# A hybrid pooling / RWKV-7 / mixture-of-experts layer on one Trainium2 core: transposes moved to VectorE in the recurrence, expert weights loaded in two halves, gathers and scatters that skip empty rows, and the first two blocks joined

## The reference, cut to what matters

```python
h = modulate(rmsnorm(x, g0), shift, scale)          # shift, scale: silu(c) @ ada_w + ada_b
p = h @ w_in                                        # pool | r, k, v, low-rank w, a, g | two gate logits
# RWKV-7 time mixing, 16 heads of 64, two directions, 256 context + 512 latent tokens:
def step(s, inp):                                   # scanned over the tokens
    sa = einsum('bhvk,bhk->bhv', s, -kk_t)
    s  = s * w_t + sa * b_t + v_t * k_t
    return s, einsum('bhvk,bhk->bhv', s, r_t)
m = (sigmoid(gp) * (pool_y @ pool_proj) + sigmoid(gr) * (rwkv_y @ rwkv_proj)) @ w_out
h = x + gate1 * rmsnorm(m, g1)
# 32 experts in 4 groups: top-1 group, top-2 experts of its 8
y = sum(gates[:, e] * ((silu(u @ w_gate[e]) * (u @ w_up[e])) @ w_down[e]) for e in range(32))
out = h + gate2 * rmsnorm(y, g3)
```

## Time and profile before

| | us |
|---|---|
| three runs | 1523.47, 1524.66, 1525.41 |
| median | 1524.66 |
| the profiled execution | 1523.53 |
| its span (first to last instruction) | 1521.0 |

### The profile page before, as it was taken

How to read it: one execution, slowest core, us unless ns; L and a number is a source line. 1 busy time by engine, 2 the same in 40 slices (tenths; PEclk the granted TensorE clock), 3 DMA queues, 4 the chain that set the end, 5 groups by cost and what they waited for, 6 DMA issues and landing times. The chain is left out here.

```text
span 1521.0 us, 37771 instructions
## 1 busy us (share of the span) xinstructions
PE 1328.0 (87%) x16500; PEld 797.3 (52%) x16500; DVE 620.2 (41%) x974; ACT 578.9 (38%) x964; POOL 235.3 (15%) x191
## 2 busy tenths in 40 slices
PE   5889999999999999999998788999999468788780
PEld 3445555554888888888887233444445323222220
DVE  1247777674555445454444451523321510000014
ACT  4235445542665656556654530000003223322233
POOL 0011111220322333333330000000000011100002
PEclk9999999999999999999999899999999679989895
DMA  9204565645222222112200529453454659999984
GB/s 379 90 1 139 159 174 177 185 123 177 106 86 73 100 67 84 67 71 83 80 29 23 229 99 387 161 202 112 152 219 186 275 214 422 426 424 425 426 341 186
DMA packets 104697, 279.87 MB, mean 184 GB/s; under 512 B 20691, under 2 KB 69971, under 8 KB 90595
## 3 DMA queue, kind: packets, MB, share of 16 engines
q1 hardware_dynamic: 98596, 248.24, 44.0%
q0 software_dynamic: 5952, 29.36, 4.9%
HBM read 232.48 MB, written 53.49 MB: 188 GB/s over the span
## 5 line engine op out<-in xcount | busy, mean ns | idle before, releaser
L391 PE MATMUL pr_ps<-hT,pr_w 128*128 128x512 f32 x384 | 172.2, 602 | 4.0 <-DVEq L99 4.0
L972 DVE COPY_PREDICATED rc_T<-masks_sb,rc_ps 128x512 f32<-128x512 uint32 x96 | 65.2, 728 | 151.2 <-PE rc_ps L761 151.1
L391 PEld LDWEIGHTS pr_ps<-hT,pr_w 128*128 128x128 f32 x384 | 72.1, 191 | 94.9 <-issue 90.1
L1250 PE MATMUL mg_ps<-hT,mg_w 128*128 128x512 f32 x256 | 112.9, 600 | 2.7 <-PEq L1029 2.7
L1737 DVE TENSOR_TENSOR mg_w<-mg_w,ex_pgu 128x256 f32<-128x256 f32 x16 | 6.7, 421 | 194.5 <-ACT mg_w L1731 194.5
L1250 PEld LDWEIGHTS mg_ps<-hT,mg_w 128*128 128x128 f32 x256 | 49.1, 192 | 65.4 <-issue 65.4
L1269 ACT ACTIVATE mg_sig<-mg_ps 128x512 f32<-128x512 f32 x16 | 9.6, 597 | 188.1 <-PE mg_ps L1250 188.1
L761 PE MATMUL rc_ps<-rc_T,rc_Z 64*64 64x64 f32 x3840 | 73.4, 221 | 6.6 <-issue 5.3
L912 ACT ACTIVATE rc_G<-rc_ps 128x512 f32<-128x512 f32 x120 | 66.1, 599 | 23.5 <-PE rc_ps L761 23.0
L501 POOL TENSOR_TENSOR pr_kd<-pr_rate,pool_space 128x768 f32<-128x768 f32 x16 | 29.0, 1814 | 280.9 <-DVE pr_kraw L543 280.9
L734 PE MATMUL rc_ps<-masks_sb,rc_T 128*128 128x128 f32 x480 | 67.6, 281 | 4.8 <-DVE rc_Tf L970 4.8
(11 more groups left out here) (358 smaller groups left out, 2596.7 us busy)
## 6 DMA issues: line engine op xcount, KB each, us to landing
bonus_sb<-in_ada_w SPq DMA_DIRECT2D x16, 1024.0 KB, 7.0
mg_w<-in_w_merge SPq DMA_DIRECT2D x8, 1792.0 KB, 7.5
pr_w<-in_w_prep SPq DMA_DIRECT2D x8, 1664.0 KB, 9.8
kr_chunks<-pr_KR SPq DMA_DIRECT2D x16, 768.0 KB, 4.2
bk_chunks<-pr_BK SPq DMA_DIRECT2D x16, 768.0 KB, 6.5
rc_BK<-bk_chunks SPq DMA_DIRECT2D x24, 512.0 KB, 4.2
rc_KR<-kr_chunks SPq DMA_DIRECT2D x24, 512.0 KB, 4.2
rwkv_y<-in_w_experts SPq DMA_DIRECT2D x5, 2048.0 KB, 17.8
```

What stands on the lines that cost most here:

```text
L391: last = pe.matmul(lat_bank[:, :], wv[:, j * KT + kt, :], hT[:, kt, lat], start=(kt == 0), stop=(kt == KT - 1))
L972: dve.copy_predicated(T[u][:, d, :, :, :].rearrange("p q b t -> p b q t"), level(int(s[1:]), d), by_side).then_inc(dve_s, 1)
L1250: last = pe.matmul(ps[u][j][:, :], w[:, u, w0 + k, :], rhs, start=(k == 0), stop=(k == n - 1))
```

## The change

Three places are changed.

1. `begin` and `low_rank_inputs` become one block. Only the identity is loaded ahead of `ada_w`; the other masks come last. `ada_w` comes in four pieces by rows of the sum (each with all 2,048 columns), so each piece feeds 8 products into four groups of 32 PSUM partitions. One transpose round and one copy bring the columns; the low-rank products start as soon as the first part of `hT` is modulated; and `prepare`'s first loads are issued right behind.
2. In the recurrence T is turned by DVE (`Tt`, one transpose of 128 partitions for d = 0, two of 64 partitions that also swap the halves for d = 1), at every level. The Tr units are gone from PE and ACT. G and X (up to b = 16) and U are made for both directions interleaved. ACT copies both halves of U (DVE copied one before). The turn of V moves behind U.
3. The experts' gate/up and down weights have semaphores of their own and are loaded separately; indirect DMAs carry a bound, and empty rows have an index beyond it; results are scaled by their gate in ACT's copy and scattered to one of two rows per token, so that the end reads them with 8 plain DMAs from SP. The spill loop is entered only if there is a spilled tile. The 8 MB fill is gone.

```diff
@@ begin @@
+                sp.dma_start(g["masks"][:, 0:1, :], I["masks"][:, 0:1, :]).then_inc(ident_loaded, 16)
+                for i in range(PIECES):
+                    sp.dma_start(w[:, i, :, :, :].rearrange("p n k c -> p n (k c)"),
+                                 I["ada_w"][0:NF, :, i * KP:(i + 1) * KP, :].rearrange("n p k c -> p n (k c)")).then_inc(w_loaded[i], 16)
...
+                first_loads(sp)
+                sp.dma_start(g["masks"][:, 1:, :], I["masks"][:, 1:, :]).then_inc(masks_loaded, 16)
...
+                for i in range(PIECES):
+                    pe.wait_ge(w_loaded[i], 16)
+                    for k in range(KP):
+                        for n in range(NF):
+                            pe.matmul(ps[2 * H * n:2 * H * n + 2 * H, :], lhs[:, i * KP + k, :], w[:, i, n, k, :], start=(i + k == 0), stop=False)
@@ recurrence_units @@
-        out += front("G2") + front("Tr1") + front("Vt") + back("P")[0:1] + front("X2") + back("P")[1:2]
-        out += front("G4") + front("Tr2") + back("XTr") + front("X4") + back("U")
-        out += front("G8") + front("Tr4") + back("Y") + front("X8") + back("S") + rows_of(0, 1)
-        out += front("G16") + front("Tr8") + rows_of(2) + front("X16") + rows_of(3)
-        out += front("G32") + front("Tr16") + ahead("BKt") + front("X32")
+        out += front("G2") + back("P")[0:1] + front("X2") + back("P")[1:2]
+        out += front("G4") + back("XTr") + front("X4") + back("U") + front("Vt")
+        out += front("G8") + back("Y") + front("X8") + back("S") + rows_of(0, 1)
+        out += front("G16") + rows_of(2) + front("X16") + rows_of(3)
+        out += front("G32") + ahead("BKt") + front("X32")
@@ recurrence @@
+            by_dve += [("T1", i, d // 2), ("Tt2", i, d // 2)]
+        if s in ("X2", "X4", "X8", "X16") and d == 1:
+            by_dve += [(f"Tt{2 * int(s[1:])}", i, 0), (f"Tt{2 * int(s[1:])}", i, 1)]
...
+                        act.activation(UV[u][0:HD, d, 1::2, :, :], turned[0:HD], ACT.Copy)
+                        act.activation(UV[u][HD:P, d, 0::2, :, :], turned[HD:P], ACT.Copy).then_inc(act_s, 1)
...
+                        for half, to in ((slice(0, P), slice(0, P)),) if d == 0 else zip(OWN, OWN[::-1]):
+                            last = dve.transpose(Tt[u][to, d, :, :, :].rearrange("p q b t -> p (q b t)"), T[u][half, d, :, :, :].rearrange("p q b t -> p (q b t)"))
@@ experts @@
+                for p in range(PAIRS - 2):
+                    sp.wait_ge(s["gu"], p + 1)
+                    for n in (2 * p + WSLOTS, 2 * p + WSLOTS + 1):
+                        if n < NE:
+                            gate_up_of(n)
+                    if p:
+                        sp.wait_ge(s["down"], p)
+                        for n in (2 * p + WSLOTS - 2, 2 * p + WSLOTS - 1):
+                            if n < NE:
+                                down_of(n)
...
+                for t in range(NT):
+                    for j in range(2):
+                        sp.dma_start(got[t][j], g["y_dram"][j * SEQ + t * P:j * SEQ + t * P + P, :]).then_inc(gath[t], 16)
```

486 lines of the change are left out of this document (238 added, 248 removed).

## The result

| | before | after |
|---|---|---|
| median of four runs, us | 1524.07 | 1557.34 (1549.71 to 1572.26) |
| ratio, with its 95% interval | | 1.0234 (1.0156 to 1.0312) |
| the profiled execution | 1523.53 | 1556.44 |
| its span | 1521.0 | 1554.6 |
| mean granted clock of PE | 0.944 | 0.917 |

The account below looks back on a forecast made before the run. Bounds: a start waiting for data, a PE-bound recurrence, a DMA-bound expert stream with a serial end. Terms -11.6 + 30 + 0.9 - 5.6 - 15.5 - 11.6 = -13.4 gave 1511 us; forecast's range 1495 to 1527, wider range 1482 to 1537.

Parts of the forecast that it names:

- The recurrence: Recurrence: DVE and ACT queues replace PE as bound; chunks of 40.5 us latent, 37.3 context; +30 us.
- The layout: Recurrence: step-by-step schedule of one latent chunk over PE, ACT and DVE, 39.2 us without interruptions; 36.0 for context.
- upper bound of +44: Recurrence: the loss if none of the 2 us of interruptions within units hides behind PE's waits.
- Rival 4: Recurrence: DVE and POOL block each other, T1's copies waiting beside POOL's masking; 30 us more, 1541; chance 0.16.
- Rival 1: Recurrence: PE stays the bound, so 60 us go where 30 were added; 1421; chance 0.08.
- rival 2: Recurrence comes out even: new waits swallow all interruptions, hops are shorter; 30 us less, 1481; chance 0.12.
- The start: Start: last `ada_w` piece at 32.3, low-rank products from 39.3 instead of 50.94; gain 11.6 us.
- The merge: Merge: the 8 MB fill vanishes from a PE-bound stage; nothing, or 1 us at most.
- Routing: Routing: two more DVE operations on the way to the first gather; +0.9 us.
- Experts, the stream: Expert stream: earlier reload gains 5.6, empty rows moving nothing 15.5; -28.5 with the end's part before the last pair.
- Rival 3: Experts: empty rows cost as much as full ones, so 15.5 us stay; 1527; chance 0.14.
- The end: Experts' end: later down halves, plain final reads, fewer sums; gain 11.6 in all, -4.2 after the last pair's gate/up begins.

Follow-up runs that it names:

- short waits: Parts 1 and 3 with the old recurrence, PE also waiting after X4, X8, X16 and each G of levels 2 to 32 for their copies: 1549.17 us, 1.0141.
- the version with idle products in the first chunk: Changed kernel with later POOL masks and V's turn back in level 2, plus throwaway identity products in PE's first-chunk waits: 1520.79 us, 0.9936.
- the mended new recurrence: Changed kernel with later POOL masks, V's turn back in level 2, and the state's update ahead of X16's turns on DVE: 1508.31 us, 0.9865.

## Why the prediction was wrong, point by point

**The recurrence: +72 instead of +30; this step failed.** The sign and the mechanism were right: PE stopped being the bound, waits appeared before G8 for ACT and before P, G16 and G32 for DVE, and PE's work fell by 4.5 us per latent chunk. The layout without interruptions (39.2 us) stands against 37.3 measured (30.7 of work and 6.6 of waits): it was long by 2. What failed is the line "PE waits often now, so part of the interruptions will hide; I take 1.3 of 2". The 2 us were, in the kernel before, 1.6 of interruptions and 1.5 of excess at full clock, beside a layout that was 1.1 long. The interruptions did not shrink but grew to 2.8 us, and the excess grew to 4.9, some 3 us of it by the lower clock, for which the layout had no term: 7.7 where 1.3 stood. In context chunks 7.8 stood against 1.3. Over eleven chunks that is some 81 us (the last has less), of which 14 were counted; the layout's surplus (1.9 us per latent chunk, 4.3 per context chunk) gives 29 back, and some 37 us are missing. The prediction had the very row for it: in the start it took half rate behind PE's wait for `ada_w`, by the earlier trace rows, and was right to 0.2 us (3.64 measured for 3.4). The recurrence, into which the layout put waits at every level, got no such term. Its upper bound of +44 was that of interruptions alone, and by the prediction's own terms that bound is +38.

The ends of the stretch came out worse too: the first chunk +7.0 for +4, and what follows the last X32 +4.3 for +2.

**Rival 4 (DVE and POOL block each other)** was real: 22 to 27 us for 30, by the row it named. But the layout already had T1's copy at 1.7 us, so most of it was in the forecast's own 40.5 us and didn't come on top. **Rival 1** is refuted, and **rival 2** with it: no version with the turns on DVE came down to the old period; the best had 36.7 and 39.2 us against 35.4 and 38.7. In the Trainium skill ("SBUF — State Buffer", Who interferes with whom) stands the rule that I should have weighed: a DVE instruction with two SBUF inputs contends with a GpSimd instruction that reads SBUF, and one with at most one such input doesn't. The rows agree on both halves: the copy from `rc_XT`, mask and data in SBUF, takes 0.75 us or, beside POOL, 1.74 in the median; that from PSUM (L986) 0.68 to 0.76 all along.

**The start: -7.8 for -11.6 by the traces, -8 to -10 by the runs.** The order of events was right, two terms were short:

```profile
34.51 3.64 PE L247 MATMUL mod_ps<-ada_first,clhs 128*32 128x512 f32 x16 [4.64 <-DMA ada_first<-in_ada_w]
38.09 1.93 PE L250 MATMUL mod_ps<-ada_bias,ones_row 1*32 1x512 f32 x8
...
43.15 7.42 PE L263 MATMUL x_pt<-hT,lr_w 128*128 128x512 f32 x13 [1.30 <-DVE hT L216]
```

The last piece came at 34.51, not 32.3. And from the last product to the first modulation 4.3 us passed, not 3.1: the bias now takes four products, 1.93 us at half rate, where it took two and 1.07 us before. From there to `prepare` it is 33.75 us in both kernels, as forecast.

**The merge: -6.5 for 0.** "A PE-bound stage: nothing, or 1 us at most" was read from PE's busy time and not from its waits. The timeline before, PE and POOL, has this:

```profile
904.13 2.23 POOL L1259 DMA_DIRECT2D y_rows<-in_x  x4 [117.13 <-POOLq L1029]
...
952.06 1.89 PE L1235 MATMUL mg_ps<-mg_acc,masks_sb 128*32 128x512 f32 x2 [5.31 <-DVE mg_acc L1291]
```

DVE waited for a piece of `ada_w`, loaded beside the 8 MB of the fill, and PE for DVE, 5.3 us. The DMA engines stood at 0.96 from 920 to 940 us. With the fill gone the wait is gone in every version, and with it in place (the new recurrence alone) it is 5.86 us.

**Routing** +0.2 for +0.9: right.

**Experts, the stream: -19.0 for -28.5.** Rival 3 is refuted: empty rows move nothing. The software queue's line of the page, before and after (packets, MB, share):

```profile
q0 software_dynamic: 5952, 29.36, 4.9%
```
```profile
q0 software_dynamic: 4608, 8.40, 1.4%
```

29.36 MB are 16 gathers, 16 stores and the fill of 8.39 each and 4.19 of final gathers; 8.40 are half of 16 gathers and 16 scatters. That agrees with the 7 MB of the forecast within the stream. The early reload worked as well (the DMA share in the first 20 us from gate/up on is 0.78 for 0.55). What is missing is at the end. The forecast had expert 31's gate/up land first and three down halves follow it, 7.4 us. In the chain that ended last:

```profile
1468.91 39.53 DMA pl_w_box<-in_w_experts
```

This load, issued at 1468.91, took 39.5 us to land, no longer than its like at that time (median 40.9 of those issued from 1373 on). Two down halves, issued 4.6 and 6.4 us behind it, moved beside it: the second took 30.6 us and was in at 1505.9, 2.5 us ahead of the load. Loads of one queue did not wait for each other here, so the order of issue gave no order of arrival, and the 7.4 us were not won in full. The third down half was issued only at 1490.24, when its place came free, and the DMA share fell to 0.77 in the 20 us from 1489 on, where it had been 0.92 in the 20 us before the last gate/up of the kernel before. That these two together are the missing 9.5 us is my reading; no run isolates it.

**The end: -5.6 for -4.2.** From the issue of the final reads to DVE's first sum 4.9 us (1528.75 to 1533.63) where 4.3 were forecast and 8.85 stood before. DVE then waits 2.27 us for the second tile, which took part of its 2.6 back.

**The chances.** "Slower" had 0.24, mostly through rival 4. The failure was not that rival 4 was missed but that neither the layout nor any rival had a term for what PE does behind waits; 42 of the 47 us missed lie in that one stage.

**What stays open.** What an interruption is, and why it grew in the new recurrence (1.6 to 2.8 us per latent chunk, single ones up to 2.7) while it nearly vanished beside short waits (0.4), no run tells. So does why the version with idle products in the first chunk gave its 4.8 us back. And the mended new recurrence (1508 us) still has 4.4 us of excess per latent chunk and doesn't reach the old one; with a granted clock of 0.97 in these chunks only some 1.2 of the 4.4 are the lower clock, and what the rest is, beyond the 1.5 that the old one has too, stays open. So does what decides, by length, number or distance, whether idle pieces of PE bring the lower clock: the runs show cases and no rule.
